# Query, key and value projections of an encoder block by seven block products in place of eight

## The chip, the cores and the metric

One Trainium2 chip, one core of it. The metric is the device time of one execution of the program in microseconds. The kernel before takes 892.1 us, the median of three runs (890.97 to 892.67). PE is TensorE, DVE is VectorE, ACT is ScalarE, POOL is GpSimd and SP is SyncE, whose queue issues nearly all transfers.

## The reference, cut to what matters

The block takes x of 512 tokens by 1024 channels in float32, normalises it, and multiplies it by a wide matrix whose column groups feed two branches. What comes after (attention, gating, output projection, a mixture of 32 experts) is the same before and after.

```python
xn = rmsnorm(h, norm_mix_g[l])
proj = xn @ w_in[l]                       # 512 x 1024 by 1024 x 5632
zu, zv, q, k, va, ga, gb = jnp.split(proj, split_idx, axis=-1)   # 1024, 1024, 1024, 256, 256, 1024, 1024 columns
u = jax.nn.gelu(zu, approximate=False)
v = jax.nn.gelu(zv, approximate=False)
y_a = gmlp_spatial_gating(u, v, ...) @ w_branch_a[l]              # begins with a layernorm of v
att = sliding_window_attention(q, k, va, ...)
```

The change is in how the 1536 columns of q, k and va are computed, and in the layernorm of v.

## The kernel before

**Units.** The weights arrive in 34 units of 128 x 2048 values (8 KB for each partition). Units 0 to 3 (`ZV`) make v, units 4 to 7 (`Q`) the queries, unit 8 (`KVA`) the keys, unit 9 the values, units 10 to 13 (`ZU`) u, and then come the gates, branches and the output projection. A unit lands in `raw[c % 2]`. Products are wanted at nearly float32 precision, so each operand is split in two parts of a shorter type: ScalarE copies `raw` to `whi` in that type (`split_hi`, L1355), and VectorE makes `wlo = raw - whi` (`split_lo`, L1698). Both copies of 2048 elements are made one unit ahead (`start_unit`). SyncE loads unit c when unit c-2 has been split (`load_unit`, L460, L462). The same is done once for the normalised, transposed x: `xnT_hi` and `xnT_lo`, eight slices of 128 channels by 512 tokens.

**Matmuls.** A unit of q, k or va has 256 columns of the matrix over all 1024 channels. `tall_tile` (L810) makes 128 of these columns at a time: for each of the eight slices of channels, `three` (L738) multiplies hi by hi, hi by lo and lo by hi (L740, L741, L742), each a matmul of 128 x 128 weights by 512 tokens. That is 24 matmuls into one PSUM bank, and then `act_tile_done` rises. The loop of L891 runs this over the six units 4 to 9, 12 tiles, with banks 0 and 1 in turn. ScalarE copies each finished tile to `qT`, `kT` or `vaT` (L1446, L1449).

**VectorE beside it.** In the units of v it makes the attention bias table (`make_alibi`) and copies the transposed spatial weights. From unit 4 on it computes the statistics of the layernorm of v (`layernorm_stats`, L1719: two `bn_stats` and a `bn_aggr` for each of four rows of tiles, then an inverse root in twelve small steps) and then one row at a time (`layernorm`, L1731: three passes over 1024 elements). The result is first read after the first tile of u, at L914.

**Order.** Each engine runs its own instructions in the written order; semaphores alone tie the engines together. `sem >= n` waits stand ahead of the instruction that needs them. Two consecutive instructions of one engine of which the second reads the first's result also have a wait between them (`then`, L1677).

**Later.** The PE goes on through u, the gates with attention between, the output projection and the router (to about 440 us), and then through the experts, whose weights (some 200 MB) SyncE loads. Their first loads wait for tiles of the PE that free their memory (`wait_unit_used` at L511 and L516).

## Time and profile before

| | |
|---|---|
| median of three runs | 892.1 us (890.97 to 892.67) |
| profiled execution | 891.64 us |
| its span | 889.8 us |
| PE, PEld, DVE, ACT busy | 842.5, 550.6, 418.6, 238.3 us |
| mean granted TensorE clock | 0.981 |

How to read it: the span is the time from the first to the last instruction that the profiler saw, and the profiled execution is 1.84 us longer than that. A busy share is a mean over stages that have different limits, so the stage that is changed is looked at by itself. The ends of matmuls are modelled; the time from one start to the next is what a matmul costs in a stream. PEld is the loading of weights into the array, which overlaps the matmuls. An arrow in brackets names what ended an idle time.

### The profile page before, as it was taken

To read this page: it belongs to the slowest core of one execution; us is meant where nothing else is said; L and a number is where in the kernel's file an instruction comes from. 1 tells how busy PE (TensorE), PEld (TensorE's weight loads), DVE (VectorE), ACT (ScalarE), POOL (GpSimd) and SP (SyncE) were. 2 spreads that over 40 slices of the span, in tenths; PEclk is the share of its full clock that TensorE was granted. 3 is DMA by queue.
4 is the path that set the end of the run, shared out by engine and by line. 5 is a ranking of instruction groups with operands and counts; after the bars stand their busy time and mean duration, and the time that the engine had idled before them with its cause. 6 is when DMAs were issued, how large, how long until landed. Compare 5 with 4: busy or idle time off the path is not lost.

```text
span 889.8 us, 11445 instructions
## 1 busy us (share of the span) xinstructions
PE 842.5 (95%) x4631; PEld 550.6 (62%) x4631; DVE 418.6 (47%) x814; ACT 238.3 (27%) x439; POOL 6.9 (1%) x24
## 2 busy tenths in 40 slices
PE   8999999999999999999999969999985799999985
PEld 7888888887877888888834424544532443544632
DVE  5638326767765344433777335135142234235124
ACT  6332222474543222214423220101110101110114
POOL 0000000000000100000000000000000000000000
PEclk9999999999999999999999989999996999999998
DMA  8544312212122733696999999999999999999994
GB/s 295 145 94 107 103 63 94 96 48 95 53 91 69 211 107 95 255 399 245 356 371 414 421 429 426 427 428 426 428 428 427 428 429 426 430 425 424 432 406 168
DMA packets 71751, 249.49 MB, mean 280 GB/s; under 512 B 23016, under 2 KB 46608, under 8 KB 58512
## 3 DMA queue, kind: packets, MB, share of 16 engines
q1 hardware_dynamic: 71328, 247.66, 71.5%
q0 software_dynamic: 288, 1.05, 0.3%
q8 instruction: 38, 0.62, 0.3%
q14 instruction: 17, 0.14, 0.1%
q10 hardware_dynamic: 80, 0.02, 0.0%
HBM read 244.51 MB, written 4.20 MB: 280 GB/s over the span
## 4 chain that ended last, share of the span: by engine, by line
PE 85%; DMA 11%; DVE 1%; ACT 1%; issue 1%; SPq 0%; DVEq 0%; POOL 0%; ACTq 0%; POOLq 0%
PE bank L1065 17%; PE bank L740 10%; PE bank L741 10%; PE bank L742 10%; PE bank L1124 7%; DMA R<-w_down 5%; DMA R<-w_gate 5%; PE bank L767 2%; PE bank L768 2%; PE bank L769 2%; PE bank L1029 2%; PE by_side L1029 2%; PE bank L1111 2%; PE bank L1152 1%; PE bank L1153 1%; PE bank L875 1%
## 5 line engine op out<-in xcount | busy, mean ns | idle before, releaser
L1065 PE MATMUL bank<-R,packT 128*64 128x512 f32 (+1 forms) x972 | 185.2, 607 | 15.8 <-DMA R<-w_up 11.9
L1065 PEld LDWEIGHTS bank<-R,packT 128*64 128x64 f32 (+1 forms) x972 | 58.1, 128 | 125.0 <-issue 124.5
L1698 DVE TENSOR_TENSOR wlo<-raw,whi 128x2048 fp32r<-128x2048 f32 x33 | 75.5, 2288 | 84.8 <-ACT whi L1355 84.7
L740 PE MATMUL bank<-xnT_hi,whi 128*128 128x512 f32 x288 | 113.2, 393 | 0.0
L742 PE MATMUL bank<-xnT_hi,wlo 128*128 128x512 f32 x288 | 112.1, 389 | 0.0
L741 PE MATMUL bank<-xnT_lo,whi 128*128 128x512 f32 x288 | 112.1, 389 | 0.0
L1124 PE MATMUL bank<-R,actT 128*64 128x512 f32 (+1 forms) x384 | 73.8, 629 | 12.7 <-DMA R<-w_down 12.5
L1355 ACT ACTIVATE whi<-raw 128x2048 fp32r<-128x2048 f32 x33 | 63.1, 1911 | 68.0 <-PE by_side L742 33.8
L740 PEld LDWEIGHTS bank<-xnT_hi,whi 128*128 128x128 f32 x288 | 54.1, 188 | 11.4 <-issue 0.6
L742 PEld LDWEIGHTS bank<-xnT_hi,wlo 128*128 128x128 f32 x288 | 54.1, 188 | 11.3
L741 PEld LDWEIGHTS bank<-xnT_lo,whi 128*128 128x128 f32 x288 | 54.1, 188 | 10.8
L1124 PEld LDWEIGHTS bank<-R,actT 128*64 128x64 f32 (+1 forms) x384 | 22.4, 133 | 59.0 <-issue 58.4
L2200 DVE SCALAR_TENSOR_TENSOR y_lo<-bank,small,y_hi 128x512 fp32r<-128x512 f32 x26 | 19.3, 750 | 78.9 <-ACT y_hi L1573 78.9
L2209 DVE TENSOR_TENSOR h_tok<-bank,h_tok 128x512 f32<-128x512 f32 x84 | 52.2, 678 | 7.0 <-PE bank L1153 7.0
L1573 ACT ACTIVATE y_hi<-bank,small 128x512 fp32r<-128x512 f32 x26 | 17.8, 690 | 103.7 <-PE bank L1124 88.6
L2186 DVE TENSOR_REDUCE small<-bank 128x1 f32<-128x512 f32 x13 | 9.0, 690 | 73.4 <-PE bank L1082 73.3
L2192 DVE TENSOR_TENSOR act_rows<-silu_g,bank 128x512 f32<-128x512 f32 x13 | 14.0, 1077 | 62.6 <-PE bank L1065 62.6
L1568 ACT ACTIVATE actT<-by_side 128x512 f32<-128x512 f32 x13 | 7.8, 600 | 120.8 <-PE by_side L1089 120.8
L1152 PE MATMUL bank<-y_hi,onehotT 128*128 128x512 f32 x84 | 35.0, 417 | 1.5 <-ACT packT L1554 1.5
L1153 PE MATMUL bank<-y_lo,onehotT 128*128 128x512 f32 x84 | 33.0, 393 | 0.0
L1382 ACT ACTIVATE probs<-probs,small 128x128 f32<-128x128 f32 (+1 forms) x64 | 24.4, 386 | 23.1 <-DVE small L1766 23.1
L1560 ACT ACTIVATE silu_g<-bank 128x512 f32<-128x512 f32 x12 | 7.2, 596 | 81.6 <-PE bank L1065 81.6
(418 smaller groups left out, 1326.1 us busy)
## 6 DMA issues: line engine op xcount, KB each, us to landing
R<-w_up SPq DMA_DIRECT2D x27, 2048.0 KB, 22.2
R<-w_gate SPq DMA_DIRECT2D x25, 2048.0 KB, 21.5
R<-w_down SPq DMA_DIRECT2D x21, 2048.0 KB, 22.4
raw<-w_in SPq DMA_DIRECT2D x17, 1024.0 KB, 5.1
R<-w_down SPq DMA_DIRECT2D x12, 1024.0 KB, 13.8
R<-w_gate SPq DMA_DIRECT2D x14, 512.0 KB, 9.6
raw<-w_in SPq DMA_DIRECT2D x20, 256.0 KB, 4.6
R<-w_up SPq DMA_DIRECT2D x5, 1024.0 KB, 9.0
```

Of the source, the lines that this page charges most:

```text
L740: pe.matmul(dst, hi_w, hi_x, start=start, stop=False)
L741: pe.matmul(dst, hi_w, lo_x, start=False, stop=False)
L742: return pe.matmul(dst, lo_w, hi_x, start=False, stop=stop)
L1029: mm = pe.matmul(bank[PACK_BANKS[c // 2]][:, (c % 2) * 2 * P:(c % 2 + 1) * 2 * P], part[:, t, c, :], onehot[:, t, :], start=(t == 0 and pa ...
L1065: mm = pe.matmul(dst[s * w:(s + 1) * w, :], packT[:, side, c, s * w:(s + 1) * w], part_of(s, c) if part_of else slots[s // 2].tiles[s % 2] ...
L1124: mm = pe.matmul(bank[5 + n][s * w:(s + 1) * w, :], actT[:, c, s * w:(s + 1) * w], slots[s // 2].tiles[s % 2][:, c * D + n * 512:c * D + ( ...
L1152: pe.matmul(dst, onehotT[odd][:, t * P:(t + 1) * P], y_hi[:, n * 512:(n + 1) * 512], start=True, stop=False)
L1153: pe.matmul(dst, onehotT[odd][:, t * P:(t + 1) * P], y_lo[:, n * 512:(n + 1) * 512], start=False, stop=True).then_inc(line.spread_done, 1)
L1355: act.activation(whi[c % 2][:, :], raw[c % 2][:, :], ACT.Copy).then_inc(hi_split, 1)
L1382: act.activation(row, row, ACT.Exp, bias=neg_max[s % 2][:, r:r + 1], accum_out=denom[s % 2][:, r:r + 1])
L1698: dve.tensor_tensor(wlo[c % 2][:, :], raw[c % 2][:, :], whi[c % 2][:, :].bitcast(F32), ALU.subtract).then_inc(lo_split, 1)
L2209: dve.tensor_tensor(part, bank[spread_banks(line, i)[n][t]][:, :], part, ALU.add).then_inc(line.h_added, 1)
```

## The change

The six units 4 to 9 are computed by Strassen's identity in Winograd's form. A unit is a product of a 2 x 2 arrangement of weight blocks (two halves of channels j, two groups m of 128 columns) and one of x blocks (two halves of channels j, two halves h of 256 tokens). Plainly that is eight block products; the identity needs seven, of sums and differences of blocks.

- **PE.** `seven_unit(u)` makes seven products, each of four slices of channels by three matmuls of 256 tokens, 12 matmuls. Products 0, 2, 4 and 6 add into one bank (`main_psum`), product 3 has `first_psum`, 1 and 5 add into `fifth_psum`; banks alternate by unit. Between the products of `main_psum`, its state is copied out, and the next product waits for that (`part_kept`).
- **ScalarE.** `high_t` makes the hi part of four sums of x; `high_block` the hi part of each of seven 128 x 512 weight blocks of a unit (three raw, four sums), one unit ahead; `keep` copies a partial sum of 128 x 256 out of PSUM, four for each unit; one more copy writes a corner of the result.
- **VectorE.** `sum_x` makes four sums of x blocks (`tT_sum`) in ten operations on 1024 elements, `low_t` their lo parts; `sum_blocks` four sums of weight blocks for each unit (512 elements each), `low_block` the seven lo parts; `add_corner` three adds of 128 x 256 for each unit, which write the other corners. The layernorm of v takes two passes for a row in place of three, and its parts stand elsewhere: statistics of two rows in each of the first two turns, one row in each of the next three, the last row behind the loop.
- **Loads.** The same bytes; a unit's load now waits for all seven blocks of the unit two before (`units_split`). The blocks' hi and lo parts use the old `whi` and `wlo` as rings of eight, and two late homes at the end.
- Semaphores are merged (`ident_made` and `iota_made` to `pool_made`, `vecs_ready` and `eps_made` to `small_ready`, `x_reloaded` to `x_loaded[0]`), counts behind the stage are shifted by `MORE_TILES`.

The diff, cut to its core:

```diff
+            def seventh(u, b, dst, x_hi, x_lo, start):
+
+                pe.wait_ge(lo_split, Q + 7 * u + b + 1)
+                w_h, w_l = block_home(u, b, whi, late_hi), block_home(u, b, wlo, late_lo)
+                for k in range(4):
+                    pe.matmul(dst, w_h[:, k, :], x_hi[:, k, :], start=start and k == 0, stop=False, skip_group_check=True)
+                    pe.matmul(dst, w_h[:, k, :], x_lo[:, k, :], start=False, stop=False, skip_group_check=True)
+                    mm = pe.matmul(dst, w_l[:, k, :], x_hi[:, k, :], start=False, stop=k == 3, skip_group_check=True)
+                mm.then_inc(act_tile_done, 1)
...
+                seventh(u, 0, main_psum, x_block(xnT_hi, 0, 0), x_block(xnT_lo, 0, 0), True)
+                pe.wait_ge(xnT_ready, X_READY + 1)
+                seventh(u, 1, fifth_psum, tT_hi[0], tT_lo[0], True)
+                pe.wait_ge(part_kept, 4 * u + 1)
+                pe.wait_ge(xnT_ready, X_READY + 2)
+                seventh(u, 2, main_psum, tT_hi[1], tT_lo[1], False)
...
+                seventh(u, 3, first_psum, x_block(xnT_hi, 1, 0), x_block(xnT_lo, 1, 0), True)
+                pe.wait_ge(part_kept, 4 * u + 3)
+                pe.wait_ge(xnT_ready, X_READY + 3)
+                seventh(u, 4, main_psum, tT_hi[2], tT_lo[2], False)
+                seventh(u, 5, fifth_psum, x_block(xnT_hi, 1, 1), x_block(xnT_lo, 1, 1), False)
+                pe.wait_ge(part_kept, 4 * u + 4)
+                pe.wait_ge(xnT_ready, X_READY + 4)
+                seventh(u, 6, main_psum, tT_hi[3], tT_lo[3], False)
```

ScalarE's loop and the part ahead of it:

```diff
             for c in range(ZV, Q):
...
+                if c == Q - 1:
+                    high_t(0, 3)
+                    high_t(1, 5)
+                    high_t(2, 8)
+                    for b in range(4):
+                        high_block(0, b)
...
+            high_block(0, 4)
+            high_block(0, 5)
+            high_t(3, 10)
+            high_block(0, 6)
+            act.wait_ge(wsT_psum, 1)
+            for u in range(SEVENS):
+                last = u == SEVENS - 1
+                main_psum, fifth_psum = bank[u % 2], bank[4 + u % 2]
+                if not last:
+                    high_block(u + 1, 0)
+                keep(u, 0, 0, main_psum).then_inc(part_kept, 1)
...
+                    high_block(u + 1, 1)
+                keep(u, 1, 1, fifth_psum).then_inc(part_kept, 1)
+                if not last:
+                    high_block(u + 1, 2)
+                keep(u, 2, 2, main_psum).then_inc(part_kept, 1)
+                if not last:
+                    high_block(u + 1, 3)
+                    high_block(u + 1, 4)
+                keep(u, 3, 4, main_psum).then_inc(part_kept, 1)
+                if not last:
+                    high_block(u + 1, 5)
+                    high_block(u + 1, 6)
+                act.wait_ge(act_tile_done, 8 + 7 * u + 7)
+                act.activation(corner(u, 1, 0), main_psum[:, 0:2 * P], ACT.Copy).then_inc(act_tile_read, 2)
```

VectorE's:

```diff
+            def sum_x():
...
+                dve.tensor_tensor(t1, hi(0, 1), hi(0, 0), ALU.subtract).then_inc(sums_made, 1)
+                dve.tensor_tensor(part, lo(0, 1), lo(0, 0), ALU.subtract).then_inc(sums_made, 1)
+                dve.wait_ge(sums_made, 2)
+                dve.tensor_tensor(t1, t1, part, ALU.add).then_inc(sums_made, 1)
+                dve.wait_ge(sums_made, 3)
+                dve.tensor_tensor(t2, hi(1, 1), t1, ALU.subtract).then_inc(sums_made, 1)
+                dve.wait_ge(sums_made, 4)
+                dve.tensor_tensor(t2, t2, lo(1, 1), ALU.add).then_inc(sums_made, 1)
+                dve.tensor_tensor(t3, hi(1, 1), hi(0, 1), ALU.subtract).then_inc(sums_made, 1)
+                dve.tensor_tensor(part, lo(1, 1), lo(0, 1), ALU.subtract).then_inc(sums_made, 1)
+                dve.wait_ge(sums_made, 7)
+                dve.tensor_tensor(t3, t3, part, ALU.add).then_inc(sums_made, 1)
+                dve.tensor_tensor(t4, hi(1, 0), t2, ALU.subtract).then_inc(sums_made, 1)
+                dve.wait_ge(sums_made, 9)
+                dve.tensor_tensor(t4, t4, lo(1, 0), ALU.add).then_inc(sums_made, 1)
+
+            def sum_blocks(u):
...
+                dve.tensor_tensor(s1, raw_block(c, 1, 0), raw_block(c, 1, 1), ALU.add).then_inc(sums_made, 1)
+                dve.wait_ge(sums_made, T_SUMS + 4 * u + 1)
+                dve.tensor_tensor(s2, s1, raw_block(c, 0, 0), ALU.subtract).then_inc(sums_made, 1)
+                dve.tensor_tensor(s3, raw_block(c, 0, 0), raw_block(c, 1, 0), ALU.subtract).then_inc(sums_made, 1)
+                dve.wait_ge(sums_made, T_SUMS + 4 * u + 2)
+                dve.tensor_tensor(s4, raw_block(c, 0, 1), s2, ALU.subtract).then_inc(sums_made, 1)
...
+                if c == 2:
+                    sum_x()
+                if c == Q - 1:
+                    sum_blocks(0)
+                    for i in range(3):
+                        low_t(i)
+                    for b in range(6):
+                        low_block(0, b)
+                    low_t(3)
+                    low_block(0, 6)
...
+            for u in range(SEVENS):
+                last = u == SEVENS - 1
+                first_psum, fifth_psum = bank[2 + u % 2], bank[4 + u % 2]
+                if not last:
+                    sum_blocks(u + 1)
+                    low_block(u + 1, 0)
+                    low_block(u + 1, 1)
+                else:
+                    split_lo(ZU)
+                if u < 2:
+                    layernorm_stats(2 * u)
+                elif not last:
+                    layernorm(u - 2)
+                if not last:
+                    low_block(u + 1, 2)
+                    low_block(u + 1, 3)
+                dve.wait_ge(act_tile_done, 8 + 7 * u + 4)
+                add_corner(u, 0, 0, first_psum, 0)
+                if not last:
+                    low_block(u + 1, 4)
+                dve.wait_ge(part_kept, 4 * u + 4)
+                add_corner(u, 1, 1, kept[u % 2][3], 1)
+                if not last:
+                    low_block(u + 1, 5)
+                dve.wait_ge(act_tile_done, 8 + 7 * u + 6)
+                add_corner(u, 0, 1, fifth_psum, 2)
+                if not last:
+                    low_block(u + 1, 6)
+            layernorm(TT - 1)
```

## Rows read from the trace of the kernel before

**Rows 1.** The page: span, engines, rate of the transfers in 40 slices.
```profile
span 889.8 us, 11445 instructions
PE 842.5 (95%) x4631; PEld 550.6 (62%) x4631; DVE 418.6 (47%) x814; ACT 238.3 (27%) x439; POOL 6.9 (1%) x24
...
GB/s 295 145 94 107 103 63 94 96 48 95 53 91 69 211 107 95 255 399 245 356 371 414 421 429 426 427 428 426 428 428 427 428 429 426 430 425 424 432 406 168
```
**Rows 2.** Windows: busy, granted clock, DMA share, GB/s; then PE's longest wait to 420.
```profile
59.28:124.56 65.28, 65.28 (x289) 54.07 (x288) 34.33 (x42) 18.00 (x18) 0.00 (x0) 1.00 0.33 97
...
PE by_side L717 <- POOL ident L658: 1.6, 1, 1.6
```
**Rows 3.** SyncE's timeline at the first expert load; its wait; landing of unit loads.
```profile
365.45 0.36 SPq L512 DMA_DIRECT2D first_gate<-w_gate  x1
...
SPq L512 <- PE bank L742: 5.1, 1, 5.1
...
raw<-w_in SPq DMA_DIRECT2D x12, 256.0 KB, 4.3
```
**Rows 4.** PE's timeline: start, length; then a chain's piece of line 862.
```profile
59.28 0.39 PE L740 MATMUL bank<-xnT_hi,whi 128*128 128x512 f32 x1
...
124.56 0.39 PE L740 MATMUL bank<-xnT_hi,whi 128*128 128x512 f32 x1
...
563.11 0.28 PE L1029 MATMUL bank<-onehot,hn_hi 128*128 128x256 f32 x1
563.23 0.28 PE L1029 MATMUL bank<-onehot,hn_lo 128*128 128x256 f32 x1
...
205.02 1.01 PE bank L862 x8
```
**Rows 5.** DVE's timeline, 20 to 75 us; then a group (mean ns) of adds.
```profile
20.55 2.28 DVE L1698 TENSOR_TENSOR wlo<-raw,whi 128x2048 fp32r<-128x2048 f32 x1
22.75 0.75 DVE L1820 SCALAR_TENSOR_TENSOR xnT_lo<-by_side,small,xnT_hi 128x512 fp32r<-128x512 f32 x1
39.68 2.29 DVE L1698 TENSOR_TENSOR wlo<-raw,whi 128x2048 fp32r<-128x2048 f32 x1
...
64.12 1.28 DVE L1724 BATCH_NORM_STATS2 small<-v_tok 128x6 f32<-128x512 f32 x2
67.25 1.29 DVE L1724 BATCH_NORM_STATS2 small<-v_tok 128x6 f32<-128x512 f32 x2
...
70.38 0.17 DVE L1728 COPY small<-small 128x4 f32<-128x4 f32 x1
72.77 0.81 DVE L1733 TENSOR_SCALAR v_tok<-v_tok,small 128x1024 f32<-128x1024 f32 x1
73.62 1.23 DVE L1734 TENSOR_TENSOR v_tok<-v_tok,ln_g 128x1024 f32<-128x1024 f32 x1
74.88 1.22 DVE L1735 TENSOR_TENSOR v_tok<-v_tok,ln_b 128x1024 f32<-128x1024 f32 x1
...
L1795 DVE TENSOR_TENSOR wlo<-raw,whi 128x512 fp32r<-128x512 f32 x4 | 2.7, 684 | 0.0
L1775 DVE TENSOR_TENSOR attT_lo<-bank,attT_hi 128x256 fp32r<-128x256 f32 x9 | 3.8, 424 | 0.3
```
**Rows 6.** Groups of ACT: busy us, mean ns; idle before.
```profile
L1407 ACT ACTIVATE xnT_hi<-bank,small 128x256 fp32r<-128x256 f32 x6 | 2.7, 473 | 2.0 <-PE bank L725 1.8 <-DVE xnT_lo L1801 0.2
L1401 ACT ACTIVATE whi<-raw 128x512 fp32r<-128x512 f32 x4 | 2.5, 626 | 0.1
```
**Rows 7.** Pieces of the chain before and behind a long wait; windows with granted clock.
```profile
493.36 7.11 PE bank L1065 x64
...
519.51 8.43 PE bank L1124 x64
...
455.00:460.00 5.00, 4.11 (x28) 2.46 (x26) 4.07 (x12) 1.63 (x5) 0.00 (x0) 1.00 1.02 416
500.00:520.00 20.00, 12.85 (x97) 5.94 (x96) 11.64 (x15) 5.09 (x6) 0.00 (x0) 0.89 1.02 426
```

More of the change, by code:

```diff
@@ L278, in build_block @@
             landed.append((landed[c - 2] if c >= 2 else 0) + (16 * len(units[c]) if c else 0))
-        x_loaded, x_reloaded = [sem(f"x_loaded{t}") for t in range(TT)], sem("x_reloaded")
+        x_loaded = [sem(f"x_loaded{t}") for t in range(TT)]
         vecs_loaded = sem("vecs_loaded")
@@ L337, in build_block, with raw_block, block_source, block_home @@
         last_loaded = [sem(f"last_loaded{c}") for c in range(4)]
+        sums_made, part_kept, corner_ready = (sem(n) for n in ("sums_made", "part_kept", "corner_ready"))
+        SEVENS = ZU - Q
+        BLOCKS = 7 * SEVENS
+        T_SUMS = 10
+        X_READY = WIDE + KT
+        MORE_TILES = BLOCKS - 2 * SEVENS
+        RAW_BLOCK = {0: (0, 0), 3: (0, 1), 6: (1, 1)}
+        SUM_BLOCK = {1: 0, 2: 1, 4: 2, 5: 3}
+        def raw_block(c, m, j):
+            return raw_view(c, TALL)[:, 4 * j:4 * j + 4, m * P:(m + 1) * P]
+        def block_source(u, b):
+            return raw_block(Q + u, *RAW_BLOCK[b]) if b in RAW_BLOCK else s_sum[u % 2][SUM_BLOCK[b]][:, :, :]
+        def block_home(u, b, ring, late):
+            q = 7 * u + b
+            home = late[q - BLOCKS + 2][:, :] if q >= BLOCKS - 2 else ring[q % 8 // 4][:, q % 4 * 512:(q % 4 + 1) * 512]
+            return home.rearrange("p (k n) -> p k n", k=4)
+        def x_block(x, j, h):
+            return x[:, 4 * j:4 * j + 4, h * 2 * P:(h + 1) * 2 * P]
+        def corner(u, m, h):
+            tile, j = (qT, 2 * u) if u < 4 else (kT, 0) if u == 4 else (vaT, 0)
+            return tile[:, j + m, h * 2 * P:(h + 1) * 2 * P]
         ranks_psum = bank[7][:, 0:TT * NE]
@@ L822, in act_tile @@
             def act_tile(c, m, a):
[L824 removed]
+                pe.wait_ge(act_tile_read, a if 28 < a <= 36 and m == 0 else a - 2 if a == 20 else a - 1)
                 if 28 < a <= 36 and m == 1:
@@ L1437, in _ @@
                                    ACT.Gelu).then_inc(act_tile_read, 1)
[L1438 to L1449 removed]
+            high_block(0, 4)
[9 more added lines that the diff above has]
+                keep(u, 0, 0, main_psum).then_inc(part_kept, 1)
+                if last:
+                    split_hi(ZU)
+                else:
+                    high_block(u + 1, 1)
[12 more added lines that the diff above has]
+                act.activation(corner(u, 1, 0), main_psum[:, 0:2 * P], ACT.Copy).then_inc(act_tile_read, 2)
             for c in range(ZU, GA):
@@ L1717, in make_alibi, with layernorm_stats @@
                 then(dve.tensor_scalar(gate_b, gate_b, 0.5, None, ALU.mult))
-            def layernorm_stats():
+            def layernorm_stats(t0):
                 dve.wait_ge(consts_loaded, 16 * 6)
-                for t in range(TT):
+                for t in range(t0, t0 + 2):
                     dve.wait_ge(act_tile_read, 4 + t + 1)
@@ L1807, in _ @@
             dve.wait_ge(vecs_psum, 1)
-            dve.tensor_copy(small[:, 0:5 * KT], bank[0][:, 0:5 * KT]).then_inc(vecs_ready, 1)
-            dve.wait_ge(vecs_ready, 1)
+            dve.tensor_copy(small[:, 0:5 * KT], bank[0][:, 0:5 * KT]).then_inc(small_ready, 1)
+            dve.wait_ge(small_ready, 2)
             norm_x(1, 1, 2)
@@ new lines, in add_corner @@
+            def add_corner(u, m, h, src, i):
+                dve.wait_ge(part_kept, 4 * u + i + 1)
+                dve.tensor_tensor(corner(u, m, h), src[:, 0:2 * P], kept[u % 2][i][:, :], ALU.add).then_inc(corner_ready, 1)
+            def sum_x():
+                hi, lo = (lambda j, h: x_block(xnT_hi, j, h).bitcast(F32)), (lambda j, h: x_block(xnT_lo, j, h).bitcast(F32))
+                t1, t2, t3, t4 = (tile[:, :, :] for tile in tT_sum)
+                part = tT_part[:, :, :]
+                dve.wait_ge(xnT_ready, X_READY)
+                dve.tensor_tensor(t1, hi(0, 1), hi(0, 0), ALU.subtract).then_inc(sums_made, 1)
[13 more added lines that the diff above has]
+                dve.tensor_tensor(t4, t4, lo(1, 0), ALU.add).then_inc(sums_made, 1)
@@ L1835, in _ @@
                     dve.memset(wsT[HD:P, :, 0:HD], 0.0).then_inc(wsT_ready, 1)
-            for c in range(Q, ZU):
-                start_unit(c)
-                if c == Q:
-                    layernorm_stats()
-                if c - Q < TT:
-                    layernorm(c - Q)
+            for u in range(SEVENS):
+                last = u == SEVENS - 1
[4 more added lines that the diff above has]
+                    low_block(u + 1, 1)
+                else:
+                    split_lo(ZU)
+                if u < 2:
+                    layernorm_stats(2 * u)
[17 more added lines that the diff above has]
+            layernorm(TT - 1)
             for c in range(ZU, GA):
```

135 lines of the change are left out of this document (89 added, 46 removed).

## Prediction

> **What bounds the kernel now.** The page comes first [rows 1]: the PE is busy 95% of an 889.8 us span, so it is the engine to look at. The windows say where in the span the change lies. From 59.28 to 124.56 us the PE multiplies the query, key and value units: 65.28 us, the PE busy for all of it at granted clock 1.00 (the 2.4 GHz level), the DVE for 34.33 and the ACT for 18.00 [rows 2]. The third view is the list of the PE's waits up to 420 us: its longest is 1.6 us, on line 717, the first products of the program [rows 2]; none is in the stage. So whatever the PE gives up in this stage the program loses or gains in full, unless something later takes it back. Nothing later does: the big expert loads begin at 365.45, each behind a wait of SyncE for work of the PE [rows 3], and from slice 20 on the transfers run at some 425 GB/s [rows 1]. A stage that ends x us later starts that saturated stretch x us later.
>
> **The PE's own part.** Before: 12 tiles of 24 matmuls of 512 columns, the first at 59.28, the first behind them at 124.56 [rows 4]: 65.28 us, 0.227 from start to start. After: 6 units x 7 products x 12 matmuls of 256 columns, with the same 128 x 128 weights. The trace has this very form on line 1029: 0.12 us from start to start, not the 0.113 that half of 0.227 would be [rows 4]. I take 0.12 because type, weights and columns are the same: a product is 12 x 0.12 = 1.44 us, a unit 10.08, the stage 504 x 0.12 = 60.5 us. The gain is at most 4.8 us, not an eighth of 65.3 (8.2): the part of a matmul that doesn't shrink with its columns is now paid 504 times.
>
> The Trainium skill, "TensorE: Matmul & The Clock Gate", section "Back-to-back issue gap", gives N/2.4 + 2.5 ns for one isolated matmul. By that, as an estimate, 256 columns take 109 ns and the stage 55.0 us. The trace doesn't agree (120 ns), and the trace is used.
>
> **What VectorE gets.** Prices [rows 5]: a two-input operation takes 0.69 us on 512 elements, 1.23 on 1024, 2.29 on 2048; an add with one operand in PSUM takes 0.42 on 256. The next independent one starts about 0.09 before the end (two bn_stats of 0.68 in 1.28; 20.55 to 22.75 for a 2.28 us one), so the steps are 0.60, 1.14, 2.20 and 0.34. One that waits for the one before starts 0.03 to 0.04 after its end (73.62 to 74.88): 0.73 and 1.26. Taken away: six splits of 2.20 (13.2 us) and one of three passes of each layernorm. Added: ten sums over x (12.0), four low parts of them (4.6), and in each unit four block sums (0.73 + 3 x 0.60 = 2.5), seven low parts (7 x 0.60 = 4.2) and three adds (3 x 0.34 = 1.0), 7.7 a unit. That is 16.6 + 6 x 7.7 = 62.8 us where 13.2 stood. It doesn't all lie beside the PE's work: the order on the engine decides. VectorE is free at 41.88 (its split of unit 3 starts at 39.68 [rows 5], and that part is unchanged).
> - The sums over x have five independent and five dependent steps, 5 x 1.14 + 5 x 1.26 = 12.0: 53.9.
> - Block sums of unit 0, 2.5: 56.4. Three low parts of x sums, 3.4: 59.8. The first low block ends at 60.5.
> - The PE has been ready since 59.28. It starts at 60.7, the hand-over and an allowance of 0.1 for starting included: **1.4 us lost**.
> - Five more low blocks, the fourth x sum, the seventh block: unit 0's splits are through at 65.2.
> - Turn 0 of the loop: 2.5 + 4.2 + 1.0, and statistics of two rows of v, 3.13 (64.12 to 67.25 [rows 5]): 10.9, to 76.1.
> - Turn 1: the same, and the inverse root's small steps, 2.4 (70.38 to 72.77 [rows 5]): 13.2, to 89.3.
> - Turns 2 to 4: 2.5 + 4.2 + 1.0 and one layernorm in two passes, 1.26 + 1.14: 10.1 each.
>
> **Where that meets the PE.** The fifth product of a unit adds into the bank whose third state ScalarE must have copied out (part_kept). On ScalarE's queue that copy (third of the unit) stands behind the high parts of blocks 1 and 2 of the next unit, and these wait for VectorE's sums s1 and s2 of the next unit. So PE product 4 of unit u can't start before s2 of unit u+1 (0.73 + 0.69 = 1.4 after the turn begins) and some 1.1 on ScalarE (a high part, 0.63 for 512 [rows 6], a copy of 256, at most 0.47 [rows 6], and the hand-over).
> - Unit 0: wanted at 60.7 + 4 x 1.44 = 66.5; VectorE 65.2 + 1.4, ScalarE to 67.8: **1.4 lost**.
> - Unit 1: wanted 67.9 + 10.1 = 78.0; 76.1 + 2.5 = 78.7: **0.8 lost**.
> - Unit 2: wanted 88.8; 89.3 + 2.5 = 91.9: **3.1 lost**.
> - Units 3 to 5: a turn of VectorE takes 10.1, a unit of the PE 10.08. Neither waits more than 0.1 for the other.
> From 92.0 the PE has 24 products left, 24 x 1.44 = 34.6: the stage ends at **126.7** where it ended at 124.56, **2.2 us later**. As a ledger: -4.8 for matmuls, +1.4 +1.4 +0.8 +3.1 for waits, +0.3 in crumbs.
>
> **Edits costed at nothing.** ScalarE: 7 high parts, 4 copies and a corner copy are about 6.3 us of a 10.1 us unit; it is busy 18.00 of 65 us before [rows 2], and it costs only by its order, counted above. Its copies of v tiles move behind x sums; the PE asks for the first at 60.7, and they are read by 60.1. SyncE: six loads now wait for all seven blocks of the unit two before; unit 6 is asked for at 65.2 and wanted at 76.1, and a part of a load lands in 4.3 us [rows 3]. If that cover went, each late microsecond would be VectorE's and so the PE's. VectorE's split of unit 10 waits for ScalarE's, which waits for the first product of unit 5 (118.4): it is through by 122.7, and behind it stand only unit 5's adds. Layernorm 3 moves to about 129; the first product that reads it is past 132. PE waits that are met cost nothing: the 0.227 above is a mean over 12 tiles with a wait ahead of each.
>
> **The sum.** The profiled run took 891.64 us around its span of 889.8, 0.5 under the median of 892.1. 891.64 + 2.2 = 893.8; set against the median, 892.1 + 2.2 = **894.3 us**. Unknown from both sides: the PE step lies between 0.113 (half of 0.227) and 0.126 (line 862's 8 in 1.01, 64-column weights [rows 4]): stage end -0.7 to +1.6. VectorE's steps have 3% either way over 50 us: +-1.5. ScalarE's overlap (0 to 0.1): +0.3. Together 892.5 to 897.
>
> **Rivals.**
> - *VectorE keeps up.* If the sums cost less than line 1734's form says, or the PE doesn't meet them there, only the start loss stays: 59.28 + 1.4 + 60.5 = 121.2, 3.4 us sooner, 888.7. For it: inside the stage VectorE has some 63 us of work (5.4 + 10.9 + 13.2 + 3 x 10.1 + 3.2), less than the stage is long. Against it: the prices are rows of the same form, and most of the work is due in the first half. From 5 us less VectorE work before 91 us it decides. Chance 0.18. This is the side on which the kernel is not slower.
> - *Steps of VectorE don't overlap*, or each hand-over between three engines costs some 0.1 more. About 80 independent steps up to the last unit's sums x 0.085 = 6.8, and with VectorE as the bound it all goes to the end: 901. Half of it: 897.7. For it: the new stream crosses semaphores at each step. Against it: 1.28 for two and 20.55 to 22.75 [rows 5], the latter with semaphores between. Chance 0.2. The Trainium skill, "VectorE: DVE Perf Modes", section "The DRAIN you can't avoid", says that the next operation doesn't start until the pipe is empty; by that rule this rival would be the case. The trace's starts lie before the ends and don't agree.
> - *The clock falls in the new waits.* Between 500 and 520 the PE was busy for 12.85 of 20 us, the granted clock was 0.89, and the 64 matmuls from 519.51 on took 8.43 us where 64 took 7.11 before the wait [rows 7]. That is 1.3 us, 895.6. The wait of 0.89 us between 455 and 460 left it at 1.00 [rows 7]; one of 3.1 us lies between these and the 7 us of waiting there, nearer to the short ones. Chance 0.04.
> - *A wash.* The two ends of the terms cancel, within 1.8 us of the median: 0.13.
>
> **How the numbers follow.** 0.2% of 892.1 is 1.8 us, about what a measurement of this kernel can tell from no change. The likeliest case is the forecast, 0.45 (its own range 892.5 to 897, of which three tenths lie under 893.9), the rivals the rest. Slower by over 0.2%: 0.45 x 0.7 + 0.2 + 0.04 = 0.56. Same: 0.45 x 0.3 + 0.13 = 0.26. Faster: 0.18. Range 888.5 to 899: it leaves out a slice of the first rival and the far end of the second.
>
> **What would show it.** Matmuls of the new products 0.12 apart inside a product; VectorE without a gap from 41.9 to about 100; the PE's largest wait about 3 us before the fifth product of the third unit, near 89 us, put down to ScalarE's copy or VectorE's sums; the stage's end near 126.7. It is wrong if VectorE is idle in 45 to 90, if the wait at 89 is missing, or if the later stages move by another amount than this one.

## The result, and the profile of the changed kernel

The changed kernel takes 895.02 us (median of 7 runs, 894.08 to 895.43). The kernel before, on the same chip, takes 892.67 (7 runs, 890.97 to 893.73). The ratio is 1.0027 with a 95% interval of 1.0015 to 1.0039: slower by 2.35 us, with an interval of 1.3 to 3.5 us. So the two kernels do differ, but the lower end lies under the 0.2% (1.8 us) that the prediction took as a difference. The prediction was 894.3, range 888.5 to 899, slower as the likeliest. The profiled execution below took 894.08 us and is the fastest of the seven. Of the executions of the kernel before that the experiments are compared with, one took 1435.72 us at a mean granted clock of 0.555, and no ratio counts it.

The page, to be held against [rows 1]: the span is 2.3 us longer, the PE 2.8 us less busy, DVE and ACT 46 and 19 us busier.

```profile
span 892.1 us, 12113 instructions
PE 839.7 (94%) x4847; PEld 556.6 (62%) x4847; DVE 465.0 (52%) x902; ACT 257.1 (29%) x497; POOL 6.9 (1%) x24
```

The window of the stage (columns as in [rows 2]) and the PE's waits in it (us in total, times, longest):

```profile
59.28:126.81 67.53, 62.04 (x506) 60.89 (x505) 64.18 (x114) 33.90 (x70) 0.00 (x0) 1.00 0.38 106
...
PE bank L938 <- ACT kept L1527: 4.2, 3, 2.6
PE bank L938 <- DVE wlo L1954: 1.2, 1, 1.2
```

DVE is busy for 64.18 of 67.53 us. Before it was busy for 34.33 of 65.28, and the PE had no wait there. The PE's timeline (start, length, what ended the idle time) has the waits in their places: the first matmul of the stage, the first of the fifth product of each unit but the last, the last matmul of the stage and the first behind it.

```profile
60.61 0.36 PE L938 MATMUL bank<-xnT_hi,whi 128*128 128x256 f32 x1 [1.19 <-DVE wlo L1954]
...
67.66 0.38 PE L938 MATMUL bank<-tT_hi,whi 128*128 128x256 f32 x1 [1.07 <-ACT kept L1527]
...
78.54 0.39 PE L938 MATMUL bank<-tT_hi,whi 128*128 128x256 f32 x1 [0.54 <-ACT kept L1527]
...
88.91 0.28 PE L940 MATMUL bank<-xnT_hi,wlo 128*128 128x256 f32 x1
91.79 0.39 PE L938 MATMUL bank<-tT_hi,whi 128*128 128x256 f32 x1 [2.60 <-ACT kept L1527]
...
102.05 0.39 PE L938 MATMUL bank<-tT_hi,whi 128*128 128x256 f32 x1
...
112.31 0.38 PE L938 MATMUL bank<-tT_hi,whi 128*128 128x256 f32 x1
...
126.69 0.28 PE L940 MATMUL bank<-tT_hi,late_lo 128*128 128x256 f32 x1
126.81 0.40 PE L782 MATMUL bank<-xnT_hi,whi 128*128 128x512 f32 x1
```

The same five moments on DVE: the first sum of each unit's weight blocks, that is the start of each turn.

```profile
65.14 0.68 DVE L1991 TENSOR_TENSOR s_sum<-raw 128x512 f32<-128x512 f32 x1
...
76.01 0.69 DVE L1991 TENSOR_TENSOR s_sum<-raw 128x512 f32<-128x512 f32 x1
...
89.27 0.69 DVE L1991 TENSOR_TENSOR s_sum<-raw 128x512 f32<-128x512 f32 x1
89.98 0.69 DVE L1993 TENSOR_TENSOR s_sum<-s_sum,raw 128x512 f32<-128x512 f32 x1
...
99.53 0.68 DVE L1991 TENSOR_TENSOR s_sum<-raw 128x512 f32<-128x512 f32 x1
...
109.79 0.69 DVE L1991 TENSOR_TENSOR s_sum<-raw 128x512 f32<-128x512 f32 x1
```

Put the two lists side by side: 65.14 and 67.66, 76.01 and 78.54, 89.27 and 91.79, 99.53 and 102.05, 109.79 and 112.31. The PE's fifth product starts 2.52 or 2.53 us behind the start of VectorE's turn, all five times. The name behind the arrow, ScalarE's copy, is only the last link. ScalarE's own timeline around the long wait shows who is late:

```profile
90.04 0.63 ACT L1523 ACTIVATE whi<-s_sum 128x512 fp32r<-128x512 f32 x1 [5.07 <-DVE s_sum L1991]
90.58 0.37 ACT L1527 ACTIVATE kept<-by_side 128x256 f32<-128x256 f32 x1
90.84 0.62 ACT L1523 ACTIVATE whi<-s_sum 128x512 fp32r<-128x512 f32 x1
91.36 0.37 ACT L1527 ACTIVATE kept<-bank 128x256 f32<-128x256 f32 x1
```

Ahead of 90.04 it stood idle for 5.07 us, waiting for VectorE's sum s1, whose high part was next in its queue. The two copies that the PE needed (L1527, the `keep` of the change) were queued behind that. The first expert load (SyncE) is 2.28 us later than in [rows 3], as the stage's end is 2.25 later, and the span is 2.3 longer: nothing gave it back.

```profile
367.73 0.36 SPq L554 DMA_DIRECT2D first_gate<-w_gate  x1
```

### The profile page after: what moved, and what is told of

It reads as the page before. It is cut to its first block, busy times and chain, and to the rows that moved or that the text cites. A ratio compares the mean times of both kernels' runs of the same rounds, so it can differ in the third digit from the quotient of the medians.

```text
span 892.1 us, 12113 instructions
## 1 busy us (share of the span) xinstructions
PE 839.7 (94%) x4847; PEld 556.6 (62%) x4847; DVE 465.0 (52%) x902; ACT 257.1 (29%) x497; POOL 6.9 (1%) x24
## 4 chain that ended last, share of the span: by engine, by line
PE 81%; DMA 9%; DVE 7%; ACT 1%; issue 1%; SPq 0%; DVEq 0%; ACTq 0%
PE bank L1142 18%; PE bank L1201 8%; PE bank L782 7%; PE bank L784 7%; PE bank L783 7%; DMA R<-w_down 5%; DMA R<-w_gate 3%; PE bank L1106 2%; PE by_side L1106 2%; PE bank L1229 2%; PE bank L1188 2%; PE bank L811 2%; PE bank L809 2%; PE bank L810 2%; PE bank L1230 1%; DVE wlo L1954 1%
## 5 line engine op out<-in xcount | busy, mean ns | idle before, releaser
L1819 DVE TENSOR_TENSOR wlo<-raw,whi 128x2048 fp32r<-128x2048 f32 x27 | 61.8, 2288 | 46.2 <-ACT whi L1432 46.1
L782 PE MATMUL bank<-xnT_hi,whi 128*128 128x512 f32 x192 | 75.9, 395 | 0.0
L784 PE MATMUL bank<-xnT_hi,wlo 128*128 128x512 f32 x192 | 74.8, 390 | 0.0
L783 PE MATMUL bank<-xnT_lo,whi 128*128 128x512 f32 x192 | 74.8, 389 | 0.0
L1432 ACT ACTIVATE whi<-raw 128x2048 fp32r<-128x2048 f32 x27 | 51.6, 1912 | 59.1 <-PE by_side L784 33.8
L782 PEld LDWEIGHTS bank<-xnT_hi,whi 128*128 128x128 f32 x192 | 36.1, 188 | 7.6 <-issue 0.6
L784 PEld LDWEIGHTS bank<-xnT_hi,wlo 128*128 128x128 f32 x192 | 36.0, 188 | 7.6
L783 PEld LDWEIGHTS bank<-xnT_lo,whi 128*128 128x128 f32 x192 | 36.1, 188 | 7.1
```

The lines of the kernel that those rows point to most:

```text
L782: pe.matmul(dst, hi_w, hi_x, start=start, stop=False)
L783: pe.matmul(dst, hi_w, lo_x, start=False, stop=False)
L784: return pe.matmul(dst, lo_w, hi_x, start=False, stop=stop)
L1432: act.activation(whi[c % 2][:, :], raw[c % 2][:, :], ACT.Copy).then_inc(hi_split, 1)
L1819: dve.tensor_tensor(wlo[c % 2][:, :], raw[c % 2][:, :], whi[c % 2][:, :].bitcast(F32), ALU.subtract).then_inc(lo_split, 1)
```

## Experiments

Each ratio is against the kernel before, run on the same chip beside it: 891.81 us beside add_turn1, add_turn4, keep_first and ahead; 892.13 beside after_again, half_tokens, start_order and late_norm; 891.79 beside ahead_copies_behind and two_pass_norm; 892.25 beside filled_wait and after_third. A ratio is worked out from the executions of both kernels and is not the quotient of the two medians; the two differ by up to 0.5 us here. Differences in us are those of the medians unless an interval is named. As the stage begins some tenths of a microsecond earlier or later from run to run, stages are compared by their length, from their first matmul to the first one behind them.

### The price of a half-size matmul, alone

**half_tokens.** The kernel before, its tiles of units 4 to 9 made in two halves of 256 tokens: 576 matmuls, no sums, no copies.

```diff
+                if Q <= c < ZU:
+                    for h in range(2):
+                        ts = slice(h * 2 * P, (h + 1) * 2 * P)
+                        for k in range(KT):
+                            mm = three(dst[:, ts], w_h[:, k, ms], w_l[:, k, ms], xT_hi[:, k, ts], xT_lo[:, k, ts],
+                                       k == 0, k == KT - 1)
+                    mm.then_inc(done, 1)
+                    return
```

> The kernel before with one edit: each matmul of units 4 to 9 takes 256 tokens in place of 512, so there are 576 of them in place of 288, the same work in sum and nothing for VectorE. Theory: 0.12 us a matmul, 69.1 us for the stage where 65.3 stood: 3.8 us slower than before, all kept to the end. Rival (a matmul of half the columns takes half the time, 0.113): no change. Second rival (the price is that of an isolated matmul, N/2.4 + 2.5 ns = 109, by the Trainium skill's page 'TensorE: Matmul & The Clock Gate', section 'Back-to-back issue gap'): 2.4 us faster.

Measured 895.07 (894.2 to 896.11), ratio 1.0034 [1.0021, 1.0046]. The stage's first matmul and the first behind it:

```profile
58.81 0.28 PE L740 MATMUL bank<-xnT_hi,whi 128*128 128x256 f32 x1
...
127.92 0.40 PE L740 MATMUL bank<-xnT_hi,whi 128*128 128x512 f32 x1
```

69.11 us for 576 matmuls, 0.12 each, and 3.83 more than the 65.28 of before. The median rose by 2.9, and the interval (1.9 to 4.1) holds 3.8. So an eighth fewer products saves 4.8 us of PE time and not 8.2. The row of line 1029 [rows 4], from another stage, priced it rightly. By the 109 ns of the Trainium skill ("TensorE: Matmul & The Clock Gate", "Back-to-back issue gap"), which the section gives for an isolated matmul and not for a stream, this stage would as an estimate have taken 62.8 us.

### Does VectorE set the end?

**add_turn1** and **add_turn4.** Five chained statistics steps (some 3.6 us), whose result nobody reads, are put into VectorE's turn 1, ahead of the late point, or into turn 4, behind it.

```diff
+                if u == 1:
+                    dve.wait_ge(act_tile_read, 8)
+                    for _ in range(5):
+                        then(dve.bn_stats(ln_stats[:, 36:42], v_tok[:, 3, 0:512]))
```

> The changed kernel with five more bn_stats of 512 elements on VectorE in turn 1 of its loop, each waiting for the one before: 5 x 0.72 = 3.6 us that nobody needs. Theory (VectorE's list sets the time until the second sum of unit 3, about 91 us; from there the PE): each microsecond added before 91 goes to the end in full, the stage ends 3.6 us later (130.5 to 130.7 where the changed kernel has about 127), time 898.6 against 895.0. Rival A (the time lies in the matmuls of 256 columns and in ScalarE's order, VectorE has slack in the stage): under 1 us later. Rival B (VectorE bounds the whole stage): 3.6 later too; the run in turn 4 tells it from the theory.

> The same five bn_stats, 3.6 us, in turn 4 behind the layernorm row instead. Theory: at that point only unit 5's third block waits for them, which has some 3 us in hand, so 0.5 to 0.8 us later: time 895.5 to 895.8 and a wait of about 0.7 us of the PE before the third product of unit 5. Rival A: under 1 us too. Rival B (VectorE bounds the whole stage): 3.6 us later, 898.6.

add_turn1: 897.56 (897.14 to 897.88), 1.0067 [1.0053, 1.0080]; that is 5.75 over the kernel before (interval 4.7 to 7.1), some 3.4 over the changed kernel's 2.35. add_turn4: 894.97 (894.5 to 895.84), 1.0037 [1.0024, 1.0051], 0.8 over it, which by the times alone isn't clear of noise. The waits and the stage's end of add_turn1, then the same of add_turn4 behind 100 us:

```profile
PE bank L938 <- DVE wlo L1954: 4.9, 2, 3.8
PE bank L938 <- ACT kept L1527: 2.7, 3, 1.1
...
130.10 0.40 PE L782 MATMUL bank<-xnT_hi,whi 128*128 128x512 f32 x1
```
```profile
PE bank L938 <- DVE wlo L1954: 0.7, 1, 0.7
...
127.53 0.40 PE L782 MATMUL bank<-xnT_hi,whi 128*128 128x512 f32 x1
```

From its first product (60.28) the stage of add_turn1 took 69.82 us, 3.62 more than the 66.20 of the changed kernel's first profile: the work of VectorE ahead of the late point comes through whole. (The granted clock fell to 0.50 between 90 and 94 us in this execution. That cost nothing at the end, since the fifth product of unit 2 then still waited 1.15 us, and started 2.52 behind turn 2 as everywhere.) In add_turn4 the stage took 67.15 us from 60.38. Late in the stage the same 3.6 us cost 0.95: there they meet slack in the steps that only the next unit needs. That speaks for the forecast's mechanism, a deadline in the first half, and against one that counts VectorE's load over the whole stage.

### Which order decides

**start_order.** The low parts of unit 0 are made in the order in which the PE asks for them.

```diff
-                    for i in range(3):
-                        low_t(i)
-                    for b in range(6):
-                        low_block(0, b)
-                    low_t(3)
-                    low_block(0, 6)
+                    for step in (0, "t0", 1, "t1", 2, 3, "t2", 4, 5, "t3", 6):
...
```

> The changed kernel with only the order of VectorE's first low parts changed: the first low block before the low parts of the x sums, which follow one by one between the blocks. The PE can start its first product at 59.3 in place of 60.7. Theory (the end hangs on VectorE's list until unit 3's second sum): the 1.4 us comes back as a wait before the third or fifth product of unit 0, the stage ends at the same time, 0 +- 0.2 us against the changed kernel. Rival (each wait of the PE is a loss of its own): 1.4 us sooner.

894.3 (893.45 to 895.28), 1.0024 [1.0014, 1.0035]; the changed kernel, run again beside it, has 894.7, 1.0025 [1.0016, 1.0035].

```profile
PE bank L938 <- ACT kept L1527: 5.4, 4, 2.6
...
59.10 0.28 PE L938 MATMUL bank<-xnT_hi,whi 128*128 128x256 f32 x1
...
92.00:94.00 2.00, 2.00 (x11) 2.00 (x10) 2.00 (x3) 0.60 (x2) 0.00 (x0) 0.50 0.90 314
...
127.77 0.40 PE L782 MATMUL bank<-xnT_hi,whi 128*128 128x512 f32 x1
```

The PE starts 1.4 us sooner (0.22 behind the last matmul of v at 58.88, and not 1.58), the first wait is gone, and its time reappears in the later ones. The end at 127.77 is later than the 126.81 of the first profile because the granted clock fell here (0.50 in the window above). The changed kernel run beside it had the same fall, and its stage ended at 127.69. So the 1.4 us that the ledger puts down to the start can't be had back there: VectorE's turn 2 begins at 89.10, hardly sooner than 89.27.

**keep_first.** ScalarE makes the copies that the PE waits for ahead of the high parts of sums that aren't there yet.

```diff
...
                 keep(u, 0, 0, main_psum).then_inc(part_kept, 1)
...
-                    high_block(u + 1, 1)
                 keep(u, 1, 1, fifth_psum).then_inc(part_kept, 1)
-                    high_block(u + 1, 2)
                 keep(u, 2, 2, main_psum).then_inc(part_kept, 1)
...
+                    high_block(u + 1, 1)
+                    high_block(u + 1, 2)
                     high_block(u + 1, 3)
```

> The changed kernel with only ScalarE's order changed: each copy of a partial sum stands ahead of the high parts of the next unit's blocks in place of behind them; same instructions, same VectorE order. Theory: the PE's fifth product no longer waits for the next unit's sums (waits of 1.3, 0.7 and 2.9 us go), but VectorE is still late: it meets the PE at the third product of unit 2 with a wait of 2.4 us and at its seventh with 0.4. Worked out from the changed kernel's rows: stage end 2.5 us sooner, 892.5. Rival (VectorE's total alone sets the end, and the order on ScalarE only names the place of the wait): 0 to 0.5 sooner, 894.5 to 895.

891.31 (890.62 to 892.89), 0.9998 [0.9989, 1.0007]. No wait for ScalarE is left, only VectorE's:

```profile
PE bank L938 <- DVE wlo L1952: 3.4, 2, 2.2
...
88.00:90.00 2.00, 2.00 (x12) 2.00 (x11) 1.97 (x5) 0.35 (x1) 0.00 (x0) 0.50 0.00 0
...
124.66 0.40 PE L782 MATMUL bank<-xnT_hi,whi 128*128 128x512 f32 x1
```

The PE now waits ahead of 85.69 (2.2 us) for the low part itself; the wait of 0.4 expected at the seventh product is not listed. The clock fell behind that wait too (the window above), so the stage is to be held against the profiles of the changed kernel with the same fall: 64.44 us from 60.22, where those have 67.32 and 67.31. The order on ScalarE's queue alone was worth some 2.9 us of stage. In time it was worth 2.85 us by the medians and 2.6 by the ratios, the whole loss, and some more than the 2.5 expected.

**late_norm.** Only VectorE's layernorm work is moved: statistics of one row in each of turns 1 to 4, the root and all four rows' normalisation from turn 5 on.

```diff
-                if u < 2:
-                    layernorm_stats(2 * u)
-                elif not last:
-                    layernorm(u - 2)
+                if 1 <= u < 5:
+                    layernorm_stats(u - 1)
+                elif last:
+                    layernorm_root()
+                    layernorm(0)
+                    layernorm(1)
...
+            layernorm(2)
             layernorm(TT - 1)
```

> The changed kernel with VectorE's statistics and layernorms moved later, one row's statistics in each of turns 1 to 4, the inverse root and two rows in turn 5, two rows behind the loop; same instructions, ScalarE untouched. Theory: VectorE is some 5 us sooner at unit 3's sums, so of the four waits only the first two (1.3 and 1.3) stay and the seven products end near 122.6, 4.3 us sooner; but the normed rows are now late for the first product that reads them (a wait of about 2.2 us at some 130 us), so 2 us sooner in sum: 0.2 to 0.5 over the kernel before. Rival (the sum of VectorE's work sets the time wherever it stands): within 0.5 of the changed kernel.

892.98 (891.77 to 893.57), 1.0012 [1.0003, 1.0021].

```profile
PE bank L991 <- DVE v_tok L1857: 2.4, 1, 2.4
PE bank L938 <- DVE wlo L1953: 1.2, 1, 1.2
PE bank L938 <- ACT kept L1527: 1.1, 1, 1.1
...
122.28 0.40 PE L782 MATMUL bank<-xnT_hi,whi 128*128 128x512 f32 x1
```

The stage now ends 2.3 us sooner than before, and the first reader of the layernorm waits 2.4: the gain is given back right behind the stage. The time is 0.85 us over the kernel before. The interval, 0.3 to 1.9 us, holds most of the 0.2 to 0.5 expected, so the difference from the forecast isn't clear of noise.

**ahead.** Both orders together: ScalarE's of keep_first, and on VectorE the sums over x right behind the split of unit 2, statistics of rows 0 and 1 ahead of unit 0's fifth block, rows 2 and 3 in turn 0, the root alone in turn 1, and the copy of the spatial weights in the last turn. The high part of the fourth x sum moves ahead of unit 0's blocks on ScalarE.

```diff
-                if c == 2:
+                if c == 1:
                     sum_x()
...
+                    for b in range(4):
+                        low_block(0, b)
+                    for i in range(4):
+                        low_t(i)
+                    layernorm_stats(0)
+                    layernorm_stats(1)
+                    for b in range(4, 7):
+                        low_block(0, b)
...
+                if u == 0:
+                    layernorm_stats(2)
+                    layernorm_stats(3)
+                elif u == 1:
+                    layernorm_root()
...
+                else:
+                    copy_spatial()
```

> The changed kernel with the same instructions on every engine in another order: copies first on ScalarE as in the run before; on VectorE the sums over x begin right after the split of unit 2 (into the idle time before the spatial weights arrive), the copy of the spatial weights moves to the last turn, statistics of two rows stand before unit 0's fifth block, those of the other two in turn 0, the inverse root in turn 1. Theory: VectorE is then some 6 us ahead, the PE never waits, and only its own sum is left: 504 x 0.12 = 60.5 us from 59.3 to 119.8, 7.1 us sooner than the changed kernel and 4.7 sooner than the kernel before, all of it kept to the end: 887.9. Rival A (the PE is paced by something else in these products, or the saving is taken back by the expert loads): the stage ends near 120 but the time stays at 890 or above. Rival B (matmuls slow down when the waits go, clock or port): the step rises over 0.12.

886.96 (886.74 to 887.96), 0.9951 [0.9937, 0.9964]: 4.85 us faster than the kernel before by the medians, 4.4 by the ratio, with an interval of 3.2 to 5.6; some 7 us faster than the changed one. The PE has no wait in the stage.

```profile
59.00 0.28 PE L938 MATMUL bank<-xnT_hi,whi 128*128 128x256 f32 x1
...
119.47 0.40 PE L782 MATMUL bank<-xnT_hi,whi 128*128 128x512 f32 x1
```

60.47 us are 504 x 0.12, the term of the forecast's sum and nothing beside it. The same arithmetic on the same engines loses 2.35 us in one order and gains 4.4 to 4.85 in another.

**ahead_copies_behind.** The same with ScalarE's copies in their old order.

> The kernel of the run ahead, but with ScalarE's copies of partial sums behind the high parts of the next unit again, as in the changed kernel. It tells how much of what ahead gained over the changed kernel is VectorE's order alone. Theory: VectorE is early enough that the copies behind cost little: waits of 0.4 and 0.3 us and the hand-overs with them, the stage 1.2 us longer than in ahead (61.7 in place of 60.5), about 888.1 where ahead had 887.0, 3.6 to 3.8 us under the kernel before. Rival (ScalarE's order is what costs): most of the gain of keep_first over the changed kernel (2.9 us) is lost again, 1.9 under the kernel before.

888.06 (887.73 to 888.53), 0.9955 [0.9942, 0.9969], the stage from 58.88 to 120.66, 61.78 us. With VectorE on time ScalarE's order costs 1.3 us of stage, where it cost 2.9 with VectorE late. The times alone don't separate this run from ahead, as their intervals overlap. Against the changed kernel, VectorE's order (with the high part that moves ahead of it) alone brings 5.8 us: 1.4 at the start, and 4.4 of stage (66.20 to 61.78).

**two_pass_norm.** The kernel before with nothing changed but the layernorm's two passes for three.

```diff
-                then(dve.tensor_scalar(row, row, ln_mv[:, 2 * t:2 * t + 1], rstd[:, t:t + 1], ALU.subtract, ALU.mult))
-                then(dve.tensor_tensor(row, row, ln_g[:, :], ALU.mult))
-                dve.tensor_tensor(row, row, ln_b[:, :], ALU.add).then_inc(ln_ready, 1)
+                then(dve.scalar_tensor_tensor(out=row, in0=row, scalar=ln_mv[:, 2 * t:2 * t + 1], in1=ln_g[:, :],
+                                              op0=ALU.subtract, op1=ALU.mult))
+                dve.scalar_tensor_tensor(out=row, in0=row, scalar=rstd[:, t:t + 1], in1=ln_b[:, :],
+                                         op0=ALU.mult, op1=ALU.add).then_inc(ln_ready, 1)
```

> The kernel before with one part of the change alone: each row's layernorm in two passes of VectorE in place of three. Theory: VectorE idles beside a PE that waits for nothing in this stage, so the 0.7 us saved in each of four rows moves nothing: ratio 1.000 within 0.001. Rival (work of VectorE in this stage reaches the end in the kernel before too): up to 2.8 us faster.

891.46 (890.02 to 892.97), 0.9998 [0.9989, 1.0007]: the shorter layernorm is worth nothing by itself, as VectorE is then on nobody's path.

### The clock

**after_again** and **after_third** are the changed kernel, profiled anew. In both the granted clock fell behind the long wait.

> The changed kernel itself, unaltered, timed beside the other runs of this call: 2.2 to 2.5 us over the kernel before of the same chip (ratio 1.0025 to 1.0028). It is the base for start_order and late_norm.

> The changed kernel unaltered once more, beside filled_wait: 2.2 to 2.5 us over the kernel before. Its profile shows whether the granted clock falls behind the 2.6 us wait as in after_again, or not, as in the first profile of this kernel; theory: either can be, the wait is the same each time and the stage takes 66.2 us without the fall and 67.3 with it. Rival (the fall belonged to one chip or one build): it is not seen.

894.7 (891.99 to 895.96) and 894.81 (893.75 to 895.79), ratios 1.0025 [1.0016, 1.0035] and 1.0027 [1.0017, 1.0037]. Windows of after_again:

```profile
90.00:92.00 2.00, 0.46 (x2) 0.46 (x3) 2.00 (x4) 2.00 (x6) 0.00 (x0) 0.88 0.83 231
92.00:94.00 2.00, 2.00 (x11) 2.00 (x11) 2.00 (x3) 0.53 (x2) 0.00 (x0) 0.50 0.84 293
94.00:96.00 2.00, 2.00 (x15) 2.00 (x14) 1.97 (x4) 0.90 (x2) 0.00 (x0) 0.77 0.00 0
96.00:98.00 2.00, 2.00 (x19) 2.00 (x18) 2.00 (x5) 0.93 (x3) 0.00 (x0) 1.00 0.00 0
...
92.35 0.41 PE L938 MATMUL bank<-tT_hi,whi 128*128 128x256 f32 x1
92.57 0.41 PE L939 MATMUL bank<-tT_lo,whi 128*128 128x256 f32 x1
...
127.69 0.40 PE L782 MATMUL bank<-xnT_hi,whi 128*128 128x512 f32 x1
```

At 0.50 (the 1.2 GHz level) the matmuls start 0.21 to 0.22 apart (92.35 to 92.57), where 0.12 is what they take at 1.00. The shares of the windows add up to 3.4 us at 0.50. The stage took 67.32 us here (60.37 to 127.69) and 67.31 in after_third, against 66.20 in the first profile, where the clock stayed at 1.00 through the same wait: 1.1 us.

**filled_wait.** 20 products of the identity on the PE, whose result nobody reads, ahead of the fifth product of unit 2.

```diff
+                if u == 2:
+                    pe.wait_ge(wsT_ready, 1)
+                    for _ in range(20):
+                        pe.matmul(bank[7][:, 0:P], ident[:, :], ident[:, :], start=True, stop=True)
```

> The changed kernel with 20 products of the identity with itself (128 x 128, into a bank that nobody reads) on the PE ahead of its wait before the fifth product of unit 2, where it stands idle for 2.6 us; they take about 20 x 0.11 = 2.2 us and leave 0.4 us of waiting. VectorE's and ScalarE's work is the same. Theory (this wait lets the granted clock fall to the 1.2 GHz level for some 3.3 us in part of the executions, and that costs about 1.1 us there): the granted clock is 1.00 from 88 to 98 us, the stage takes 66.2 to 66.4 us from its first product, and the time is that of the changed kernel's better executions, 0.3 to 1.1 us under its median. Rival (the fall comes from something else, such as the seven-product stream as a whole): the clock falls there all the same, in profile and time nothing changes.

895.01 (893.6 to 896.2), 1.0029 [1.0020, 1.0039].

```profile
89.13 4.63 PE L963 MATMUL bank<-ident 128*128 128x128 f32 x40
93.51 0.36 PE L938 MATMUL bank<-tT_hi,whi 128*128 128x256 f32 x1
...
92.00:94.00 2.00, 2.00 (x20) 2.00 (x20) 2.00 (x3) 0.86 (x2) 0.00 (x0) 1.00 0.95 334
```

The clock stays at 1.00. But the filling took 4.4 us, twice what I had meant, and overran the wait by 1.6 us (the fifth product starts at 93.51, where turn 2 at 89.36 and 2.52 us make 91.88). The stage took 67.44 us, no less than with the fall, and the time is that of the changed kernel beside it: the 0.3 to 1.1 us expected didn't come. It hardly tells what makes the clock fall either. Two of the seven executions with an unfilled wait kept the clock as well, so one filled execution that kept it is weak evidence. That the idle time is the cause stays open, and so does what the fall costs in the timed runs.

## Why the prediction was right, point by point

| step | forecast | measured |
|---|---|---|
| matmul of 256 columns | 0.12 | 0.12 |
| VectorE: block sums of unit 0 begin | 53.9 | 53.84 |
| first low block | 59.8 | 59.78 |
| PE starts | 60.7 | 60.61 |
| turns 0, 1, 2 begin | 65.2, 76.1, 89.3 | 65.14, 76.01, 89.27 |
| fifth product of unit 2: wanted, got | 88.8, 91.9 | 89.03, 91.79 |
| stage ends | 126.7 | 126.81 |
| layernorm 3 done | 129 | 128.5 |
| longest wait of the PE | 3.1 | 2.6 listed, 2.88 between two starts |

- **The PE's own part** held: 0.12, shown by half_tokens and by the 60.47 us of ahead.
- **VectorE's stream** held to 0.1 us over 50 us, since nearly all its prices came from rows of the same forms. Behind 41.87 its first listed idle time in the stage is 0.46 us, at 120.59. Its steps overlap as the trace before said: below, two blocks of 0.68 in 1.29, and each next one starts 0.07 to 0.09 before the end of the last, with semaphores in between.

```profile
60.39 1.29 DVE L1954 TENSOR_TENSOR wlo<-s_sum,whi 128x512 fp32r<-128x512 f32 x2
61.59 0.69 DVE L1954 TENSOR_TENSOR wlo<-raw,whi 128x512 fp32r<-128x512 f32 x1
62.19 1.29 DVE L1954 TENSOR_TENSOR wlo<-s_sum,whi 128x512 fp32r<-128x512 f32 x2
```

- **One price was too low.** I took the two passes of the layernorm at the price of a plain two-input operation, 1.23. With one more operand, a scalar for each partition, they take 1.28 (below), 2.52 for the two steps and not 2.40. That is 0.12 of the 0.16 by which turns 2 and 3 are longer than forecast (89.27 to 99.53 to 109.79: 10.26, not 10.1). So the sentence on units 3 to 5, that neither engine waits more than 0.1 for the other, fell short: the PE's fifth products of units 2, 3 and 4 also stand 10.26 apart (91.79, 102.05, 112.31), where its own work is 10.08. That is 0.36 us in two turns. The end was only 0.1 off, since the fifth product of unit 2 came 0.1 to 0.2 sooner than forecast and the last 14.5 us as worked out. Errors of opposite sign met here, which is luck. (92.0 and 34.6 make 126.6; the prediction wrote 126.7.)

```profile
L1856 DVE SCALAR_TENSOR_TENSOR v_tok<-v_tok,small,ln_g 128x1024 f32<-128x1024 f32 x4 | 5.1, 1278 | 0.0
```

- **A small wait wasn't foreseen.** The third product of unit 2 starts at 86.09, 0.38 and not 0.12 behind the matmul before it; VectorE's low part for it is through at 85.94. So the fifth is wanted at 89.03 and not 88.8. It cost nothing, as the date at 91.79 stood behind it, but it is the place where keep_first then waits.
- **The ledger adds up but doesn't come apart.** Its entries (1.4 at the start, 1.4, 0.8, 3.1) read as if each could be saved. start_order saved the first, and the time stayed. In the order as changed one date sets the end, VectorE's turn 2 at 89.27, with 2.52 us through ScalarE and 24 products behind it.
- **Passing to the end.** Stage +2.25, first expert load +2.28, span +2.3. ahead shows the same in the other direction: stage end 5.1 sooner, time 4.4 to 4.85 less.
- **VectorE keeps up** (0.18) didn't happen in the order as changed. The run ahead shows it reached by order alone: VectorE is busy for 19.70 us between 20 and 41.88, where it was busy for 15.61 in the changed kernel, its turn 0 begins at 62.23 and not at 65.14, and the stage takes the 60.5 us that this rival counts with.
- **Steps don't overlap** (0.2) fell with the rows above. The rule that the prediction took from the Trainium skill ("VectorE: DVE Perf Modes", "The DRAIN you can't avoid"), that the next operation starts only when the pipe is empty, isn't borne out by them. The same section adds that an operation that isn't held starts earlier. With that the rows agree, so the section doesn't stand for this rival as the prediction has it.
- **The clock falls** (0.04) was priced about rightly, 1.3 against 1.1 us, and given too small a chance. I placed the wait nearer to one of 0.9 us that left the clock alone than to the 7 us that didn't. Of seven profiled executions with a PE wait of 2.2 to 3.8 us in this stage, five show the fall. The forecast had no such fall, and the one profile of the changed kernel that matches it to 0.1 us, the fastest execution of seven, had none. In the two other profiles of the changed kernel the stage took 1.1 us longer. The mechanism was right, but that the stage's end came out so close is in part luck too. The times bear the forecast of +2.2 out less finely: +2.35, +2.57 and +2.56 us in three comparisons.
- **A wash** (0.13): the interval excludes no change, but its lower end, 0.15%, lies under the 0.2% of the rival. The repeats, 1.0025 and 1.0027, lie at the same place.

## What to carry to other kernels

Fewer multiplications on the busiest engine are paid with additions on the next one, and it wasn't that engine's load over the stage that decided here but the date by which its first half is due: lay its steps out one by one, with the durations of the same forms, against the dates at which the bound engine asks for them. A copy on which the bound engine waits shouldn't stand in a queue behind work that waits for a late third engine. Ask of a ledger of waits which single date they all hang on, since removing a wait ahead of that date gains nothing.

## What the hardware showed unexpectedly

- The granted clock fell to 0.50 for about 3.4 us behind PE waits of 2.2 to 3.8 us, in five of seven profiled executions (after_again, after_third, start_order, add_turn1, keep_first; not in the first profile of the changed kernel, nor in add_turn4, with the same wait of 2.6). A wait of 2.4 us right behind the stage, in late_norm, left it at 1.00 as well. What decides between the two stays open, and so does how many of the timed runs had it.
- Behind a wait the second matmul starts 0.20 to 0.22 after the first and not 0.12 (60.61 to 60.81, 91.79 to 92.01): each wait costs 0.1 us more than its length.
- A 128 x 128 product of plain float32 operands is two instructions of 0.11 us, 0.22 in all (the 40 of filled_wait), twice what I had set for it (4.4 us for the 20 products).
